# Operand rows of every K tile at 208 bytes into their block, in a two-block transformer kernel

## What is computed

```python
z = h @ w_in                                  # q, k, v, gates and convolution input
h = h + y @ w_out
h = h + (silu(h @ w_gate) * (h @ w_up)) @ w_down
...
g = x @ w_in_2                                # q, k, v, u and two gates
merged = sigmoid(gate_attn) * (o_attn @ w_branch_attn) + sigmoid(gate_pool) * (p @ w_branch_pool)
x = layer_norm(ALPHA * x + merged @ w_out_2)
x = layer_norm(ALPHA * x + square(relu(x @ w_ff1)) @ w_ff2)
```

## Time and profile before

| | |
|---|---|
| median of the runs | 2449.94 us (2449.77 to 2450.12) |
| the profiled execution's own time | 2449.89 us |
| its span, first to last instruction | 2447.8 us |
| TensorE busy, matmuls | 2433.8 us, 14762 matmuls |
| VectorE busy | 1614.5 us |
| ScalarE busy | 1202.2 us |
| HBM traffic over the span | 183 GB/s |

### The profile page before, as it was taken

One profiled execution on the slowest core, in us unless ns is written; L12 is line 12 of the kernel. 1 busy time (PEld: TensorE's weight loads), 2 busy tenths in 40 slices (PEclk: granted clock), 3 DMA queues, 4 the chain that ended last, 5 costly groups with the idle time before them and its releaser, 6 DMA issues.

```text
span 2447.8 us, 36417 instructions
## 1 busy us (share of the span) xinstructions
PE 2433.8 (99%) x14762; PEld 2173.7 (89%) x14762; DVE 1614.5 (66%) x2518; ACT 1202.2 (49%) x1728; POOL 173.9 (7%) x195
## 2 busy tenths in 40 slices
PE   8999999999999999999999999999999999999999
PEld 8999998888888888888888888888998888888887
DVE  5646676676666666667677756678885665565667
ACT  6545545544544543455555654544554443443544
POOL 0001111000000000002211102031110000000010
PEclk9999999999999999999999999999999999999999
DMA  7554456666566666665655455565566666656663
GB/s 250 180 161 139 141 165 189 200 184 194 182 198 190 189 190 189 192 190 185 197 188 167 166 185 190 184 193 186 162 196 193 189 189 189 194 190 189 183 193 117
DMA packets 125751, 449.59 MB, mean 184 GB/s; under 512 B 13840, under 2 KB 16400, under 8 KB 125584
## 3 DMA queue, kind: packets, MB, share of 16 engines
q1 hardware_dynamic: 125296, 446.91, 58.8%
q10 hardware_dynamic: 288, 0.36, 0.0%
HBM read 445.12 MB, written 2.10 MB: 183 GB/s over the span
## 4 chain that ended last, share of the span: by engine, by line
PE 96%; DVE 2%; ACT 1%; issue 0%; DMA 0%; ACTq 0%
PE out_bank L614 28%; PE out_bank L618 27%; PE out_bank L615 14%; PE out_bank L617 14%; PE out_bank L622 3%; PE out_bank L621 3%; PE out_bank L623 3%; DVE w_lo L1307 1%; ACT w_hi L895 0%; PE side_bank L734 0%; PE side_bank L694 0%; PE side_bank L749 0%; PE side_bank L725 0%; DVE h L1824 0%; DMA h<-in_tokens 0%
## 5 line engine op out<-in xcount | busy, mean ns | idle before, releaser
L1307 DVE TENSOR_TENSOR w_lo<-raw,w_hi 128x1024 fp32r<-128x1024 f32 x839 | 1037.4, 1240 | 601.0 <-ACT w_hi L895 596.9
L895 ACT CAST w_hi<-raw 128x1024 fp32r<-128x1024 f32 x840 | 878.1, 1049 | 953.6 <-PE out_bank L618 874.8
L614 PE MATMUL out_bank<-a_op,w_hi 128*128 128x512 f32 x1984 | 784.2, 395 | 0.5 <-DVE h L1334 0.3
L618 PE MATMUL out_bank<-a_op,w_hi 128*128 128x512 f32 x1984 | 776.7, 391 | 0.0
L615 PE MATMUL out_bank<-a_op,w_lo 128*128 128x256 f32 x1984 | 558.8, 282 | 0.0
L617 PE MATMUL out_bank<-a_op,w_lo 128*128 128x256 f32 x1984 | 552.0, 278 | 0.0
L617 PEld LDWEIGHTS out_bank<-a_op,w_lo 128*128 128x128 f32 x1984 | 380.1, 192 | 84.3
L615 PEld LDWEIGHTS out_bank<-a_op,w_lo 128*128 128x128 f32 x1984 | 372.9, 188 | 77.0
L614 PE MATMUL out_bank<-b_op,w_hi 128*128 128x512 f32 x992 | 389.7, 393 | 0.0
L618 PE MATMUL out_bank<-b_op,w_hi 128*128 128x512 f32 x992 | 388.0, 391 | 0.0
L614 PEld LDWEIGHTS out_bank<-a_op,w_hi 128*128 128x128 f32 x1984 | 373.1, 188 | 2.0 <-DVE w_lo L1307 0.7
(11 more groups left out here) (302 smaller groups left out, 1974.6 us busy)
## 6 DMA issues: line engine op xcount, KB each, us to landing
raw<-in_w_ff SPq DMA_DIRECT2D x256, 512.0 KB, 4.2
raw<-in_w_in SPq DMA_DIRECT2D x223, 512.0 KB, 3.7
raw<-in_w_gu SPq DMA_DIRECT2D x176, 512.0 KB, 4.2
raw<-in_w_down SPq DMA_DIRECT2D x88, 512.0 KB, 4.3
raw<-in_w_out SPq DMA_DIRECT2D x64, 512.0 KB, 4.3
raw<-in_w_ba SPq DMA_DIRECT2D x16, 512.0 KB, 3.9
raw<-in_w_bp SPq DMA_DIRECT2D x16, 512.0 KB, 3.8
out<-h SPq DMA_DIRECT2D x8, 256.0 KB, 2.3
```

What stands on the lines that cost most here:

```text
L614: t_.e.matmul(bank[:, :], wh, a_both, start=start, stop=False, skip_group_check=True)
L618: mm = t_.e.matmul(bank[:, :], wh, a_both, start=False, stop=stop, skip_group_check=True)
L895: a.e.copy(w_hi[:, m % SPLIT, :], raw[:, u % RAW, :]).then_inc(hi_split)
L1307: v_.e.tensor_tensor(w_lo[:, m % SPLIT, :], raw[:, u % RAW, :], w_hi[:, m % SPLIT, :].bitcast(F32), ALU.subtract).then_inc(lo_split)
```

## The change

The blocks of both operand tensors grow from 1088 to 1152 elements (4352 to 4608 bytes). The first K tile of a block begins at element 52 in place of 48 (208 bytes in place of 192), the second at element 628 (2512 bytes) in place of 564 (2256 bytes). The low row follows the high row by 258 elements as before. `a_op` for the first mixer is a view on the front of the larger room and keeps its layout. To make room, the scratch that the program reserves at the beginning of each partition for dynamic DMAs is set to 8192 bytes; the default, used before, is 16384.

```diff
--- before.py
+++ after.py
@@ -194,12 +194,13 @@
             return ctx.enter_context(nc.semaphore(name))
 
 
-        ROW, PLACE = SEQ + 2, 48
+        ROW, PLACE, PLACES = SEQ + 2, (52, 628), 1152
         TAIL = slice(96, P)
         h = sb("h", [P, KT, TOK])
-        a_op = sb("a_op", [P, KT, 2, TOK], F32R)
-        a_late = a_op[:, :, :, :].rearrange("p k i t -> p (k i t)").rearrange("p (m c) -> p m c", m=KT // 2)
-        b_op = sb("b_op", [P, KT // 2, 4 * TOK], F32R)
+        a_room = sb("a_room", [P, KT // 2 * PLACES], F32R)
+        a_op = a_room[:, 0:KT * 2 * TOK].rearrange("p (k i t) -> p k i t", k=KT, i=2)
+        a_late = a_room[:, :].rearrange("p (m c) -> p m c", m=KT // 2)
+        b_op = sb("b_op", [P, KT // 2, PLACES], F32R)
         raw = sb("raw", [P, RAW, UNIT])
         w_hi = sb("w_hi", [P, SPLIT, UNIT], F32R)
         w_lo = sb("w_lo", [P, SPLIT, UNIT], F32R)
@@ -222,7 +223,7 @@
         acc2 = sb("acc2", [P, SEQ])
         csum = turn_tab[H8, 0:TOK]
 
-        last_slot = b_op[:, KT // 2 - 1, PLACE + 2 * ROW:PLACE + 4 * ROW]
+        last_slot = b_op[:, KT // 2 - 1, PLACE[1]:PLACE[1] + 2 * ROW]
         cneg, pick = last_slot[:, 0:TOK], last_slot[:, TOK:TOK + HEADS]
         cq = sb("cq", [P, 2, HEADS])
         gms = sb("gms", [P, KT, 2])
@@ -239,16 +240,16 @@
 
         def part(op, kt, i, n=SEQ):
 
-            at = PLACE + ROW * (2 * (kt % 2) + i)
+            at = PLACE[kt % 2] + ROW * i
             return op[:, kt // 2, at:at + n]
 
         def parts(op, kt, n=SEQ):
-            at = PLACE + ROW * 2 * (kt % 2)
+            at = PLACE[kt % 2]
             return op[:, kt // 2, at:at + 2 * ROW].rearrange("p (i t) -> p i t", i=2)[:, :, 0:n]
 
         def affine_column(i, x):
-            rows = b_op[:, :, PLACE:PLACE + 4 * ROW].rearrange("p m (o i t) -> p m o i t", o=2, i=2)
-            return rows[:, :, :, i, SEQ + x]
+            at = ROW * i + SEQ + x
+            return b_op[:, :, at + PLACE[0]:at + PLACE[1] + 1:PLACE[1] - PLACE[0]]
 
         def bank_of(t):
             return out_bank[t.n % OUT_BANKS]
@@ -2171,7 +2172,7 @@
     arrays |= {"in_tokens": tokens, "in_params": params, "in_consts": con, "in_mask1": mask1,
                "in_mask2": mask2, "in_positions": positions}
     arrays = {n: np.ascontiguousarray(x) for n, x in arrays.items()}
-    nc = bacc.Bacc("TRN2", target_bir_lowering=False, num_devices=1)
+    nc = bacc.Bacc("TRN2", target_bir_lowering=False, num_devices=1, dynamic_dma_scratch_size=8192)
     aps = {n: nc.dram_tensor(n, x.shape, mybir.dt.from_np(x.dtype), kind="ExternalInput").ap()
            for n, x in arrays.items()}
     out = nc.dram_tensor("out", (P, KT, SEQ), F32, kind="ExternalOutput").ap()
```

## The result

The changed kernel takes 2500.32 us at the median of two runs (2497.02 and 2503.61) against 2449.94: ratio 1.0205, 95% interval 1.0181 to 1.023. It is 50 us slower, outside the predicted range of 2431 to 2451; that it is slower is clear, whether by more than two per cent is not, as the interval has 1.02 inside. The profiled execution is the one of 2497.02 us, with a span of 2494.9 us.

A forecast was written before the change was run, and what follows sets the result against it. The prediction took TensorE to bound the kernel: number of matmuls times the distance between their starts. Its terms summed as 2449.9 - 14.2 - 0.3 + 0.4 = 2435.8 us, say 2436, with a range of 2431 to 2451.

The forecast's parts named there:

- The count of 2848: Quads (four products of an even and an odd K tile) that run in the changed layout: 2848.
- (a): Even K tiles moved to 208 bytes take the odd tiles' durations: 5 ns less a quad, 14.2 us gained.
- the signs set down beforehand: In ff1 afterwards: L614 391, L615 278, L617 278, L618 391 ns; load beside L615 188; 128 quads in 88.1 us.
- "no change" rival: Place isn't the cause, perhaps the weight load beside is: no or partial change, 2441 to 2451 us, chance 0.22.
- (b): The affine stage's 128 even K-tile products gain 0 to 6 ns each: 0.3 us taken.
- (c): Where VectorE or ScalarE arrives last, TensorE's gain is waited away: 0.4 us lost.
- (d): Halved DMA scratch costs nothing and only makes room; tensors behind it keep their places modulo 256 bytes.
- the slower one: Even long product clashes with the weight tile read beside it: 7 ns a quad, 2452 to 2475 us, chance 0.07.
- The larger gain: All four products fall to the trace's lowest durations: 17 ns a quad, 2402 to 2432 us, chance 0.09.

The follow-up runs named there:

- 192 and 192: The changed kernel with even and odd K tiles both at 192 bytes: 2486.06 us, ratio 1.0147 to the kernel before.
- 208 and 192: The changed kernel with even K tiles at 208 bytes and odd ones at 192: 2468.01 us, ratio 1.0073 to the kernel before.
- first map: Loop of only the paired products, 256 pairs of even and odd places in 16-byte steps, weights unmoved: mean 702.8 ns a quad, one case 680.0.

## Why the prediction was wrong

What bounds the kernel was right: the time is the number of quads times their distance, and nearly all of the loss is in that distance. The count of 2848 held up: 13.3 x 2848 = 38.0 us for 192 and 192 against a measured 36.4, 6.67 x 2848 = 19.0 for 208 and 192 against 18.3.

The step that failed is (a), "I take for every even tile what the odd one shows in the same stretch", which was to bring 5 ns a quad and cost 20.0 and 13.3. It treats a product's duration as a property of its own row's place. The even short product was to fall from 282 to 278 and, in the first regime, went to 284; the odd tile's, which kept their place modulo 256 bytes, rose from 278 to 288 and from 391 to 399. Even the sentence that seemed to make it safe, that L617 had "both itself and its successor at 208", left out the product ahead and the weight loads under both. With the weights moved by 96 bytes the short products of the same rows take 276 and 275. None of the signs set down beforehand fits: the weight load beside L615 did go from 192 to 188 ns, as it should (L618's load in the trace after), and the product above it got longer all the same. The load that went up in the first regime, from 188 to 193 ns, was that of the odd tile's long product.

The evidence was in the prediction, misread. The k stage gave 292 and 287 ns for two products of one row at one place. I read that stage as "places are worth some ns"; it says that one place has different prices, according to what goes ahead or is loaded beside it. The q stage, where the odd tile's products are the longer ones and not the even's as in ff1, could be read either way. The load of 192 ns beside L615 was noticed and given to the "no change" rival.

Step (b), 0.3 us gained in the affine stage, rested on one pair of K tiles; that stage takes 96.0 us before and 96.3 after. Step (c) was right in kind and turned round in sign: about 2 us of the loss don't reach the span, part of them because two waits for VectorE are gone. Step (d) was right and is shown: scratch and room 1.000.

The rival that came true is the slower one, a clash between the moving row and the weight tile read beside it, by their distance. Its mechanism is shown by moving the weights alone and by moving both. Its price was too small: it priced 7 ns a quad from the q stage, the steady regimes cost 20.0 and 13.3. The larger gain, "every row in one relation to the loads", exists too, at another place. It asked for 2 x 388 + 2 x 275 and the kernel with moved weights shows 389, 276, 275 and 388. The range's upper end of 2451 stood on the no-change case, with 0.07 for all slower outcomes up to 2475 us and 0.01 above 2499, where the median came to lie. In the first map only four of 256 pairs of places beat the old kernel's, so a loss was the likely outcome.

The page TensorE: Matmul & The Clock Gate of the Trainium skill, section "Wait — 56ns, not 53.3ns?", gives 2.5 ns over the columns' time for a product. Here the best quad is 40 ns over 640, 10 a product, and the worst steady one of this kernel 18. By the Trainium skill's page SBUF — State Buffer, section "SBUF: two separate sides", TensorE never waits for another engine at its ports. These runs agree: the loop without the other engines and the kernel with them take the same distances. But the two reads of TensorE itself, row and weight tile, aren't independent in these runs.

Three things stay open. Why the distance acts in this way is not shown: the maps have grains of 32 bytes, but no run looked at where they come from. What exactly makes the stream change its regime wasn't tried beyond the pauses of the loops; that it can is shown. And that the two runs of the changed kernel, 6.6 us apart, differ by the share of the two regimes is only argued, as the slower one has no trace; 1022 quads at 6.67 ns more would be 6.8 us.

## What to carry to other kernels

When one engine streams two operands at once, don't price an address from a row of the old trace: a place is worth what its distance to everything read beside it makes of it. Map the relation in a small loop that runs the products alone, then move one operand in the whole kernel; here the loop gave back the four distances that the kernel had shown, 693, 700, 707 and 713 ns, and then named three beforehand, 680, 680 and 707, which the kernel followed. A duration without spread that changes between two stages at equal places is a sign of such a dependence. And where the old layout sits in a good place, as here, a fresh one will more often lose than gain.

## What the runs showed of the hardware

- The steady distances of fp32r quads fall mostly on a ladder of 6.67 ns (185 of 256 cases of the first map within half a nanosecond): 680.0, 693.3, 700.0, 706.7, 713.3 ns for the same 1536 columns, 5% between the first and the last with nothing else changed than addresses within 256 bytes.
- Weight tiles moved alone change the time (2500 to 2414 us in the kernel, by 96 bytes). Rows and weight tiles moved together by a multiple of 32 bytes keep it in three of four pairs of places (the fourth varies by its start); by 16 they don't (693.3 to 706.7 in the loop, 2450 to 2487 us in the kernel).
- One set of places can have two steady regimes (713.3 and 706.7 ns), held for hundreds of microseconds; a change was seen after side products and after a start that was 0.03 us late.
- The fastest version found keeps the order and work of the kernel and takes 2414.5 us, ratio 0.9856, by placement alone.
